# Decode attention of a hybrid decoder step: value products of two groups placed between the two halves of every second scoring

## The chip, the cores and the metric

One core of one Trainium2 chip runs the whole kernel. The metric is device time in microseconds (us); a profiled execution also has a span, from its first to its last instruction. All inputs and outputs are fp32.

## The reference, cut to what matters

The kernel computes one step of a one-layer decoder for a prompt of 1024 tokens and for 8 sample sequences of 8 new tokens each. The change touches only the latent attention of the samples. Each sequence reads 32 cache pages of 128 tokens (latent width 256, rotary width 32) through a page table, and its queries are 8 heads x 8 tokens = 64 rows:

```
def one_seq(args):
    pt, ql, qr, cn, kn = args
    ckv = concatenate([cache_ckv[layer, pt].reshape(4096, 256), cn])
    kr  = concatenate([cache_kr[layer, pt].reshape(4096, 32), kn])
    scores = (einsum("bqhc,btc->bhqt", ql, ckv) + einsum("bqhr,btr->bhqt", qr, kr)) * MLA_SCALE
    p = softmax(where(mask, scores, NEG_INF))
    return einsum("bhqt,btc->bqhc", p, ckv)
```

## The kernel before, in words

`decode_attention` (L1433) runs on all engines between the prompt's cross-attention and the samples' cross-attention (`cross_decode`). It takes the 256 pages of the 8 sequences as 64 **groups** of 4 pages, 8 groups (G) to a sequence, numbered n = 0 to 63. PE's program, L1585 to L1616, is written out by hand as 16 **steps** of 4 groups each (S = 4), n = 0, 4, ..., 60. A step scores groups n to n+3, and works off the values of the four groups from p = n - 8 on, that is of the sequence before. Two steps make a sequence: the steps with n a multiple of 8 (p % G == 0), below called **first steps**, and the others, below called **second steps**, which are the ones that the change rewrites.

The parts of PE's program:

- `scores(n, part)` (L1523): for each of 8 slices of the latent (d, 32 wide) 8 matmuls on 32x64 tiles of the array (L1535), so 64 for a half (4 slices) and 128 in all; then 16 matmuls for the rotary part (L1543), and in a second step also 4 + 2 recorded ones for the new tokens (L1549, L1550). They all add up in PSUM banks 0 to 3, and the last one raises `scored`. The first half waits for the transposed queries (`q_in`), for the scores of the step before to be out of PSUM (`s_done`) and for the turned keys (`keys_done`), L1528 to L1530.
- `turn_probs(p)` (L1553): 4 transposes (L1559) of the probabilities of groups p and p+1. It waits for their exponentials (`exped`) and for its PSUM bank (5 or 6, `pt_done`).
- `values(n)` (L1563): 4 products in the code, 8 matmul records, on L1575 (probabilities x latents, 256 columns), which add up in bank 7 (bank 0 for the last sequence) and raise `pv_done`. `pair(p)` is two of them, so 16 records; for the first pair of a sequence 2 more on L1572.
- `turn_side(j)` (L1505): the transposes of the new tokens' probabilities (L1510) and of the output of the sequence before (L1519); it waits for the first exponential of the sequence.

The order in a first step is: half of the scoring, `turn_side`, `turn_probs(p)`, the other half, `turn_probs(p + 2)`, `pair(p)`, `turn_probs(p + 4)`, `pair(p + 2)`. In a second step: all of the scoring, `turn_probs(p + 2)`, `pair(p)`, `pair(p + 2)`. In steps 0 and 4 there are no values yet. After step 60 PE goes on with `turn_side(7)` and the values of the last sequence (L1600 on).

Around it:

- DVE: `keep_scores` (L1694) takes the four groups out of PSUM (L1704) once `scored` is up, and after a second step takes the row maximum (L1712 to L1727), which raises `maxed`; `keys` (L1680) turns the latents of later groups (L1032, L1041) as their pages land.
- ACT: `exps` (L1642, instructions L1649) makes the exponentials in place after `maxed`; `probs` (L1634, L1639) copies turned probabilities out of PSUM; `finish` (L1652, L1655) takes a sequence's output out once all its values are done (`pv_done`), ahead of the exponentials of the next sequence in ACT's queue.
- POOL (L1803): after the scoring of step n it gathers the pages of groups n+8 to n+11, one indirect DMA of 512 KB each (`gather_pages`, L1057), and then two groups' rotary keys (`gather_rotary`, L1076). The first gather waits for `scored` of step n; each page gather also waits for `pv_done` of the group whose slot it overwrites (19 slots).
- SP (L1480): the other rotary keys, the queries of the sequence after next, and at the end the first loads of the stages behind, after `scored` or `pv_done`.

Of the kernel before, what the change touches and what calls it, by code (L numbers as in the profile page):

```python
# [990 lines left out]
G = NPAGES // 4  # L991
# [31 lines left out]
def key_slot(n):  # L1023

    return (n + S) % (2 * S)
# [407 lines left out]
def decode_attention(nc, ps, a, k, at, e, late, clear_old):  # L1433
# [3 lines left out]
    NB = KVL // 32  # L1437
# [16 lines left out]
    def probs_at(p):  # L1454

        return 5 + p // 2 % 2, pt[:, p // 2 % 2]
# [7 lines left out]
    with ExitStack() as c:  # L1464
# [39 lines left out]
        def _(pe):  # L1504
            def turn_side(j):  # L1505

                if j:
                    pe.wait_ge(side_kept, j)
                pe.wait_ge(exped, j * (G + 1) + 1)
                last = pe.transpose(ps[0:NS, SIDE, 0:R], sn[:, j % 2, :], k["ident"][0:R, 0:R])  # L1510
                if 0 < j < DECB - 1:
                    last = turn_out(j - 1)
                last.then_inc(side_turned, 1)
# [9 lines left out]
            def scores(n, part):  # L1523
                b, new = n // G, n % G == G - S
                x = key_slot(n)
                cols = lambda i, f: ps[f * R:(f + 1) * R, i, 0:S * 64].rearrange("p (x w a) -> p x a w", x=S, a=2)
                if 0 in part:
                    pe.wait_ge(q_in[b % 2], 64 * (b // 2 + 1))  # L1528
                    pe.wait_ge(s_done, item(b, n % G))
                    pe.wait_ge(keys_done, n // 2 + 2)  # L1530
                for d in part:
                    for f in range(2):
                        for i in range(4):
                            rows = slice(32 * i, 32 * (i + 1))
                            pe.matmul(cols(i, f), q_rows[rows, b % 2, d, :],  # L1535
                                             kT[rows, x:x + S, 2 * f:2 * f + 2, d, :], start=(d == 0), stop=False,
                                             tile_position=(32 * i, f * R))
                if NB - 1 not in part:
                    return
                for f in range(2):  # L1540
                    for i in range(4):
                        rows = slice(32 * i, 32 * (i + 1))
                        last = pe.matmul(cols(i, f), qrope[rows, b, :], rT[rows, x:x + S, 2 * f:2 * f + 2, :],  # L1543
                                         start=False, stop=not (new and i == 0 and f == 0),
                                         tile_position=(32 * i, f * R))
                if new:
                    o = ps[0:R, 0, S * 64:S * 64 + NS]
                    for t in range(CT):
                        pe.matmul(o, qlat[:, t, b, :], k["cnT"][:, t, :], start=False, stop=False)  # L1549
                    last = pe.matmul(o, qrope[0:ROPE, b, :], k["krT"][:, :], start=False, stop=True)  # L1550
                last.then_inc(scored, 1)

            def turn_probs(p):  # L1553

                pe.wait_ge(exped, p // G * (G + 1) + 3 + p % G)
                if p >= 4:
                    pe.wait_ge(pt_done, p // 2 - 1)
                for w in range(4):
                    last = pe.transpose(ps[:, probs_at(p)[0], w * P:(w + 1) * P], sc[:, (p + w // 2) % NSC, w % 2:HK:2],  # L1559
                                        k["ident"][:, :])  # L1560
                last.then_inc(p_turned, 1)

            def values(n):  # L1563
                b, g = n // G, n % G
                pe.wait_ge(pt_done, n // 2 + 1)
                to, held = acc(b), probs_at(n - n % 2)[1]
                if g == 0:
                    pe.wait_ge(side_kept, b + 1)
                    if 0 < b < DECB - 1:

                        pe.wait_ge(o_normed, b)
                    pe.matmul(ps[0:R, to, 0:KVL], ptn[:, b % 2, :], k["cn"][:, :], start=True, stop=False)  # L1572
                for f in range(2):
                    for e in range(2):
                        last = pe.matmul(ps[e * R:(e + 1) * R, to, 0:KVL], held[:, n % 2, f, e * R:(e + 1) * R],  # L1575
                                         raw_c[:, n % NAT, 2 * e + f, :], start=(g == 0 and f == 0 and e == 1),
                                         stop=(g == G - 1 and f == 1))
                last.then_inc(pv_done, 1)

            def pair(p):  # L1580
                values(p)
                values(p + 1)

            pe.wait_ge(cleared, 1)
            for n in range(0, NG, S):  # L1585
                p = n - LAG
                if p >= 0 and p % G == 0:
                    scores(n, range(NB // 2))
                    turn_side(p // G)
                    turn_probs(p)  # L1590
                    scores(n, range(NB // 2, NB))
                else:
                    scores(n, range(NB))
                if p >= 0:
                    turn_probs(p + 2)
                    pair(p)
                    if p % G == 0:
                        turn_probs(p + 4)
                    pair(p + 2)
            turn_side(DECB - 1)  # L1600
            turn_probs(NG - G)
            for p in range(NG - G, NG, 2):
# [1353 lines left out]
```

## Time and profile before

| | us |
|---|---|
| three runs | 1451.31, 1457.43, 1449.00 (median 1451.31) |
| the profiled execution: its own time | 1452.62 |
| the profiled execution: span | 1450.7 |
| PE busy in the span | 1392.7 (96%), mean granted clock 0.977 |
| DVE, ACT, POOL busy | 836.3, 516.0, 245.2 |
| decode_attention in the span, by PE's first and last rows | 429.5 to 665 |

The rows below are of the profiled execution, in microseconds from the span's start. A timeline row merges neighbouring instructions of one line and form: start, length to the last end, engine, line, operation, out<-in, count. Where work follows without a gap, the cost of a row is the start of the next row less its own start, since matmuls are pipelined and their ends overlap what follows.

### The profile page before, as it was taken

Reading aid. Unit: us, or ns where it says so; the run is one execution under the profiler, and the core shown is the slowest. Engines: PE = TensorE matmul, PEld = TensorE weight load, DVE = VectorE, ACT = ScalarE, POOL = GpSimd, SP = SyncE. Lnnn points to the kernel's source line nnn. Section 1 sums busy time; section 2 is a strip of 40 time slices with the busy share of each in tenths; the row PEclk is TensorE's granted clock in tenths of the full one; section 3 lists DMA queues with packets and bytes.
Section 4 is the critical chain, followed back from the end, with each engine's and each line's share of the span. In section 5 each row is a group of like instructions: output and inputs, shape, how many; then the busy total and the mean of one; then the engine's idle time right before and its main releaser. Section 6 shows DMA issues by size and latency. Waiting matters only on the chain.

```text
span 1450.7 us, 28032 instructions
## 1 busy us (share of the span) xinstructions
PE 1392.7 (96%) x11192; PEld 1218.5 (84%) x11192; DVE 836.3 (58%) x1615; ACT 516.0 (36%) x1102; POOL 245.2 (17%) x193
## 2 busy tenths in 40 slices
PE   7999999999988899898999999999999999999997
PEld 7998977777646555565999999999999999999885
DVE  3385356776676445555575676664444445567745
ACT  4321456665351222234424333443333343113100
POOL 3110037764642433410100000000000000000000
PEclk9999999999999888999899999999999999999999
DMA  6652020001372545649313113133333327452722
GB/s 235 194 158 93 1 88 1 1 1 55 130 243 65 180 147 171 214 164 380 106 44 90 45 45 89 45 90 95 106 101 115 96 93 271 167 196 72 263 87 73
DMA packets 108437, 174.37 MB, mean 120 GB/s; under 512 B 14002, under 2 KB 77298, under 8 KB 107028
## 3 DMA queue, kind: packets, MB, share of 16 engines
q1 hardware_dynamic: 98068, 136.92, 28.7%
q0 software_dynamic: 10240, 35.66, 7.2%
q8 instruction: 89, 1.46, 0.4%
q14 instruction: 40, 0.33, 0.1%
HBM read 138.49 MB, written 34.06 MB: 119 GB/s over the span
## 4 chain that ended last, share of the span: by engine, by line
PE 52%; DVE 0%; issue 0%; ACT 0%; DVEq 0%
PE ps L2462 35%; PE ps L2493 10%; PE ps L2527 6%; PE ps L2513 0%; DVE p_h L2835 0%; DVE p_h L2838 0%; DVE p_stats L2822 0%; DVE p_h L2818 0%; PE ps L2503 0%; DVE p_mv L2829 0%; ACT p_rt L2610 0%; DVE p_rs L2833 0%; DVE p_stats L2827 0%; DVE p_stats L2826 0%; DVE p_ve L2831 0%
## 5 line engine op out<-in xcount | busy, mean ns | idle before, releaser
L2462 PE MATMUL ps<-p_x,p_w 128*128 128x272 f32 x4032 | 508.7, 289 | 1.0 <-PEq L1993 0.7
L2462 PEld LDWEIGHTS ps<-p_x,p_w 128*128 128x128 f32 x4032 | 508.4, 189 | 1.5 <-issue 1.5
L2493 PE MATMUL ps<-p_uh,p_w 128*128 128x352 f32 (+1 forms) x576 | 141.9, 327 | 0.0
L987 POOL TENSOR_SCALAR p_pr<-p_pr,p_rec 128x896 f32<-128x896 f32 (+3 forms) x64 | 109.8, 1725 | 141.6 <-DVE p_rec L951 141.4
L2712 DVE TENSOR_TENSOR p_w<-p_sum,p_w 128x512 fp32r<-128x512 f32 x94 | 65.0, 691 | 119.2 <-ACT p_w L1920 119.0
L1535 PE MATMUL ps<-p_kT,p_q_rows 32*64 32x256 f32 x2048 | 104.9, 452 | 23.0 <-issue 18.7
L1535 PEld LDWEIGHTS ps<-p_kT,p_q_rows 32*64 32x64 f32 x2048 | 63.4, 157 | 60.7 <-issue 54.2
L1920 ACT ACTIVATE p_w<-p_wr 128x512 fp32r<-128x512 f32 x96 | 60.1, 626 | 131.4 <-PE ps L2493 76.0
L2493 PEld LDWEIGHTS ps<-p_uh,p_w 128*128 128x128 f32 x576 | 101.8, 188 | 0.0
L1032 DVE STREAM_TRANSPOSE p_kT<-p_rawc 128x1024 f32<-128x1024 f32 x64 | 77.7, 1232 | 38.1 <-DMA p_rawc<-cache_ckv,p_rows 37.3
L2493 PE MATMUL ps<-p_ul,p_w 128*128 128x352 f32 (+1 forms) x288 | 94.4, 328 | 0.0
L2712 DVE TENSOR_TENSOR p_w<-p_wr,p_w 128x512 fp32r<-128x512 f32 x95 | 65.6, 690 | 38.5 <-ACT p_w L1920 38.0
L1057 POOL DMA_INDIRECT p_rawc<-cache_ckv,p_rows x64 | 65.3, 1020 | 126.8 <-PE ps L1543 45.1
L1920 ACT ACTIVATE p_w<-p_sum 128x512 fp32r<-128x512 f32 x96 | 59.8, 623 | 18.5 <-PE ps L2462 11.9
L945 DVE TENSOR_REDUCE p_nmax<-ps 128x1 f32<-128x896 f32 (+3 forms) x64 | 48.1, 752 | 25.9 <-PE ps L833 24.7
L1704 DVE CUSTOM_DVE_ANT_0 p_sc<-ps,p_zero 128x256 f32<-128x256 f32 x64 | 23.3, 421 | 66.0 <-PE ps L1543 52.4
L1575 PE MATMUL ps<-p_rawc,p_pt 128*64 128x256 f32 x512 | 60.5, 384 | 0.0
L2493 PEld LDWEIGHTS ps<-p_ul,p_w 128*128 128x128 f32 x288 | 54.1, 188 | 0.0
L1639 ACT ACTIVATE p_pt<-ps 128x512 f32<-128x512 f32 x28 | 16.7, 597 | 99.3 <-PE ps L1559 99.3
L1575 PEld LDWEIGHTS ps<-p_rawc,p_pt 128*64 128x64 f32 x512 | 34.6, 137 | 20.0 <-issue 3.1
L899 ACT ACTIVATE p_pr<-ps,p_nmax 128x896 f32<-128x896 f32 (+3 forms) x64 | 47.4, 740 | 5.5 <-DVE p_nmax L945 4.7
L2546 ACT ACTIVATE p_slots<-p_slots 128x544 f32<-128x544 f32 x36 | 23.8, 661 | 70.5 <-PE ps L2462 70.5
(338 smaller groups left out, 2483.3 us busy)
## 6 DMA issues: line engine op xcount, KB each, us to landing
p_wr<-w_in SPq DMA_DIRECT2D x48, 512.0 KB, 3.6
g_kept<-p_slots SPq DMA_DIRECT2D x48, 272.0 KB, 2.5
p_ring<-g_kept SPq DMA_DIRECT2D x16, 544.0 KB, 4.3
p_x<-x_kept SPq DMA_DIRECT2D x6, 1088.0 KB, 7.5
t_kept<-p_t_raw SPq DMA_DIRECT2D x16, 272.0 KB, 2.4
p_x<-t_kept SPq DMA_DIRECT2D x4, 1088.0 KB, 8.5
p_gy<-g_kept SPq DMA_DIRECT2D x8, 544.0 KB, 5.5
p_xs<-x_prompt SPq DMA_DIRECT2D x8, 512.0 KB, 4.2
```

What stands on the lines that cost most here:

```text
L899: nc.scalar.activation(pr[:, n % PR, 0:w], src[:, 0:w], ACT.Exp, bias=nmax[:, n % PR:n % PR + 1], accum_out=tot[:, n % PR:n % PR + 1]).the ...
L945: dve.tensor_reduce(nmax[:, n % PR:n % PR + 1], src[:, 0:w], AX, ALU.max, negate=True).then_inc(maxed, 1)
L987: nc.gpsimd.tensor_scalar(pr[:, n % PR, 0:w], pr[:, n % PR, 0:w], rec[:, n % PR:n % PR + 1], None, ALU.mult).then_inc(normed, 1)
L1032: return dve.transpose(e["kT"][:, key_slot(n)].rearrange("p a d w -> p (a d w)"), e["raw_c"][:, s].rearrange("p a c -> p (a c)"))
L1057: nc.gpsimd.indirect_dma_start(e["raw_c"][:, n % NAT, :, :].rearrange("p a c -> p (a c)"), None, rows_in, bass.IndirectOffsetOnAxis(e["row ...
L1535: pe.matmul(cols(i, f), q_rows[rows, b % 2, d, :], kT[rows, x:x + S, 2 * f:2 * f + 2, d, :], start=(d == 0), stop=False, tile_position=(32 ...
L1575: last = pe.matmul(ps[e * R:(e + 1) * R, to, 0:KVL], held[:, n % 2, f, e * R:(e + 1) * R], raw_c[:, n % NAT, 2 * e + f, :], start=(g == 0 ...
L1920: nc.scalar.activation(e["w"][:, q % NW, 0], w_source(e, q), ACT.Copy).then_inc(e["w_hi"], 1)
L2462: last = pe.matmul(ps[:, lo + z, 0:PW], w[:, q % NW, part, t, :], v[:, t, z * PW:(z + 1) * PW], start=(i in STARTS and t == 0 and n == 0), ...
L2493: last = pe.matmul(ps[:, BANK_OF[g % 8], 0:tn], w[:, q % NW, part, t, :], v[:, t0:t0 + tn], start=(t == 0 and z == 0), stop=(t == KH - 1 a ...
L2527: last = pe.matmul(ps[0:r, 2 * (i % 2) + half, :], v, o[t][:, half * BANK:(half + 1) * BANK], start=(t == 0 and q == 0), stop=(t == KT - 1 ...
L2712: dve.tensor_tensor(w[:, q % NW, 1], w_source(e, q), f32(w[:, q % NW, 0]), ALU.subtract).then_inc(w_lo, 1)
```

## The change

In second steps (p >= 0 and p % G == 4) the scoring is cut into its two halves, and `turn_probs(p + 2)` and `pair(p)` stand between them; `pair(p + 2)` stays behind. Nothing else moves: first steps, steps 0 and 4, and all other engines' programs are as before. No instruction is added or taken away.

```diff
@@ -1589,14 +1589,18 @@
                     turn_side(p // G)
                     turn_probs(p)
                     scores(n, range(NB // 2, NB))
+                    turn_probs(p + 2)
+                    pair(p)
+                    turn_probs(p + 4)
+                    pair(p + 2)
+                elif p >= 0:
+                    scores(n, range(NB // 2))
+                    turn_probs(p + 2)
+                    pair(p)
+                    scores(n, range(NB // 2, NB))
+                    pair(p + 2)
                 else:
                     scores(n, range(NB))
-                if p >= 0:
-                    turn_probs(p + 2)
-                    pair(p)
-                    if p % G == 0:
-                        turn_probs(p + 4)
-                    pair(p + 2)
             turn_side(DECB - 1)
             turn_probs(NG - G)
             for p in range(NG - G, NG, 2):
```

## Rows read from the trace of the kernel before

**Rows 1.** The page: granted clock of PE in 40 slices of 36.3 us, in tenths.
```profile
PEclk9999999999999888999899999999999999999999
```

**Rows 2.** Timeline of PE, steps 56 and 60: a stretch with few gathers, then none.
```profile
632.81 1.98 PE L1535 MATMUL ps<-p_kT,p_q_rows 32*64 32x256 f32 x64
634.58 0.64 PE L1543 MATMUL ps<-p_rT,p_qrope 32*64 32x256 f32 x16
...
638.95 1.95 PE L1575 MATMUL ps<-p_rawc,p_pt 128*64 128x256 f32 x16
640.83 3.71 PE L1535 MATMUL ps<-p_kT,p_q_rows 32*64 32x256 f32 x128
644.33 0.64 PE L1543 MATMUL ps<-p_rT,p_qrope 32*64 32x256 f32 x16
```

**Rows 3.** Timeline of all engines behind the scoring of step 60.
```profile
645.53 0.74 PE L1559 MATMUL ps<-ident,p_sc 128*128 128x128 f32 x4
...
646.21 3.67 PE L1575 MATMUL ps<-p_rawc,p_pt 128*64 128x256 f32 x32
...
648.98 0.49 ACT L1649 ACTIVATE p_sc<-p_sc,p_nmax 128x256 f32<-128x256 f32 x1
...
649.81 0.24 PE L1510 MATMUL ps<-ident,p_sn 64*64 64x64 f32 x1
...
649.98 1.36 PE L1559 MATMUL ps<-ident,p_sc 128*128 128x128 f32 x8
```

**Rows 4.** Timeline of PE, second step 28, from the transposes behind step 24's scoring on.
```profile
515.45 0.75 PE L1559 MATMUL ps<-ident,p_sc 128*128 128x128 f32 x4
...
521.14 1.52 PE L1535 MATMUL ps<-p_kT,p_q_rows 32*64 32x256 f32 x29
522.97 0.37 PE L1535 MATMUL ps<-p_kT,p_q_rows 32*64 32x256 f32 x1 [0.31 <-issue]
...
525.12 4.16 PE L1535 MATMUL ps<-p_kT,p_q_rows 32*64 32x256 f32 x96 [0.15 <-issue]
529.05 0.66 PE L1543 MATMUL ps<-p_rT,p_qrope 32*64 32x256 f32 x16
...
530.27 0.75 PE L1559 MATMUL ps<-ident,p_sc 128*128 128x128 f32 x4
```

**Rows 5.** Timeline of PE, and one row of ACT, from step 20's scoring to step 24's first half.
```profile
499.17 3.67 PE L1575 MATMUL ps<-p_rawc,p_pt 128*64 128x256 f32 x32
502.78 2.10 PE L1535 MATMUL ps<-p_kT,p_q_rows 32*64 32x256 f32 x30
505.18 0.68 PE L1535 MATMUL ps<-p_kT,p_q_rows 32*64 32x256 f32 x4 [0.30 <-issue]
506.61 0.59 PE L1535 MATMUL ps<-p_kT,p_q_rows 32*64 32x256 f32 x2 [0.75 <-issue]
508.04 2.08 PE L1535 MATMUL ps<-p_kT,p_q_rows 32*64 32x256 f32 x28 [0.84 <-issue]
510.05 0.31 PE L1510 MATMUL ps<-ident,p_sn 64*64 64x64 f32 x1
...
505.20 0.47 ACT L1655 ACTIVATE p_on<-ps,p_rec 128x256 f32<-128x256 f32 x1 [5.32 <-remote]
```

**Rows 6.** Timeline of POOL: last of one series of six gathers, first and last of the next.
```profile
506.08 1.03 POOL L1076 DMA_INDIRECT p_rawr<-cache_kr,p_rows  x1 [0.30 <-issue]
516.52 1.03 POOL L1057 DMA_INDIRECT p_rawc<-cache_ckv,p_rows  x1 [9.42 <-PE ps L1543]
...
523.14 1.03 POOL L1076 DMA_INDIRECT p_rawr<-cache_kr,p_rows  x1 [0.30 <-issue]
```

**Rows 7.** Timeline of all engines, step 0: scoring beside four rotary gathers, no values.
```profile
429.45 5.14 PE L1535 MATMUL ps<-p_kT,p_q_rows 32*64 32x256 f32 x59 [1.28 <-DVE p_tots L1771]
...
434.87 3.49 PE L1535 MATMUL ps<-p_kT,p_q_rows 32*64 32x256 f32 x67 [0.28 <-issue]
```

**Rows 8.** Windows of step 24: us, busy (x) of PE, PEld, DVE, ACT, POOL, clock, DMA share, GB/s.
```profile
508.00:512.00 4.00, 3.96 (x37) 2.93 (x36) 0.03 (x1) 0.43 (x3) 0.00 (x0) 0.50 0.18 57
```

## The prediction

> **What bounds the kernel now.** I read the page first: PE is busy 96% of the span, and its clock dips only where decode_attention stands [rows 1]. So PE's program sets the end, and the question is how fast PE gets through the 16 steps. The timeline of PE where no gather runs gives clean prices. 128 scoring matmuls take 640.83 to 644.33, 3.50 us; a half of 64 takes 632.81 to 634.58, 1.77; a pair of groups' values takes 638.95 to 640.83, 1.88 [rows 2]. The 4 transposes take 645.53 to 646.21, 0.68, and two pairs of values in a row 646.21 to 649.81, 3.60 [rows 3].
>
> The same timeline in the middle is slower. In second step 28 the 128 scoring matmuls take 521.14 to 529.05, 7.91 us: 29 start at once, four come one by one some 0.7 us apart, and at 525.12 the other 96 run [rows 4]. In first step 24 the half takes 502.78 to 510.05, 7.27 us [rows 5]. No other engine is named as what ended these gaps, only "issue". POOL's rows beside them show where they come from: a series of six gathers ends at 507.11 (506.08 + 1.03), the next runs from 516.52 to 524.17 [rows 6], and PE is free 0.93 and 0.95 us after the last one ends (508.04, 525.12). I looked at eleven such steps; the gap closes 0.8 to 1.0 us behind POOL's last gather in each.
>
> The starts in those rows run ahead of the work. The last values before step 24's scoring end by 502.84 (499.17 + 3.67), yet ACT's L1655, which waits for them, starts at 505.20 [rows 5], when PE's record has 30 scoring matmuls started. So about 32 matmuls stand between the recorded start and completion when PE is held. The Trainium skill (TensorE: Matmul & The Clock Gate, the table of the array) gives a queue of 64 instructions, which would be 32 loads and 32 matmuls; the row agrees.
>
> With that I count what PE completes from the end of one scoring until it is free. Behind a first step: 515.45 to 525.12, 9.67 us; started 4 + 2 + 16 + 4 + 16 + 32 (29 + 3 single), so completed about 42. Behind a second step: from 0.68 before 499.17 to 508.04, about 9.6 us; started 4 + 32 + 36, completed about 40 [rows 5]. In clean time the first lot is worth 5.7 us and the second 4.4, but the counts agree: **while POOL issues gathers, PE is limited in matmuls, not in their length**, to 4 or 5 per us. Step 0 says the same without values and with hardly any page traffic: 59 scoring matmuls started, so about 27 completed, from 429.45 to 434.87, in 5.4 us, 5 per us [rows 7]. Under a gather a scoring matmul (0.027 us clean) costs 0.2 us; a value matmul (0.11 us) nearly the same.
>
> **The change, part by part.** It moves one `turn_probs` and one `pair` of each second step from behind `scored` to before it, in 7 steps (12, 20, ..., 60). No DMA is moved and no queue passed on SP or POOL; POOL's series starts on `scored`, so it now starts later.
>
> 1. Ahead of `scored`. Up to the first scoring matmuls of a second step nothing changes: the series behind the first step stands over the same 42 matmuls, and the held stretch ends where it did, with matmul 0 or 1 of the scoring. The moved work comes after, where nothing hides it: 0.68 + 1.88, and 0.04 for cutting the scoring (2 x 1.77 less 3.50) [rows 2, 3]: **+2.60 us** a step.
> 2. Behind `scored`. Before, 4 + 32 matmuls and the first 5 or so of the next half stood under the series. Now 16 values do, and then scoring matmuls. PE is free no earlier, since the series has the same six gathers. In the 1.07 us before POOL starts (515.45 to 516.52) [rows 4, 6] PE does some 9 values, then 8.5 us at 4 to 5 per us: 43 to 51 completed, so 27 to 35 scoring matmuls instead of 4 or 5. That is 23 to 30 fewer afterwards, at 0.027 each clean, or 0.033 as in step 24 (508.04 to 510.05 for the last 60, part of it at half clock) [rows 5]: 0.6 to 1.0, **-0.8 us**. 20 hidden values and transposes are traded for scoring matmuls that would have been short anyway.
> 3. Net +1.8 us a sequence, in the 6 second steps (12 to 52) with a series behind them (of five gathers behind step 52): **+10.8 us**.
> 4. Step 60 has no gathers. Its own sum is 2.60 less the 2.40 that leave (4.28 less 1.88): +0.2. But behind it `turn_probs(56)` needs the second group's exponential, whose instruction (648.98 + 0.49) and its accumulator read end 4.0 us after the scoring's end at 645.53. PE now comes there 4.45 us after it (649.98) and waits for nothing [rows 3]. With only 1.88 us of values and 0.17 of L1510 between, it comes at 2.05 and waits 2.0, and the transposes after it wait for later exponentials 0.5 us apart, another 0.2. **+2.2 us**, so +2.4 with its own sum.
>
> Waits that tighten elsewhere: the next first step's `s_done` wait has only 1.88 us of values in front of it, and `turn_side` the exponentials' 4.0 us; both fall under the series, where PE is held anyway, and become real only if the hold goes. `turn_probs(p + 2)` comes 1.7 us or more earlier but its exponentials are made before the scoring starts, so nothing. DVE keeps its order; its keys land with the gathers, ahead of use.
>
> Sum: +13.2 us on the profiled execution's 1452.6, 1465.8. The median of the runs shown is 1.3 lower, so **1464.5 us**. The bounds of part 2: at worst nothing is got back (2.60 a sequence, +18 in all, 1469); at best everything that left counts (0.2 a sequence, +3.6 in all, 1455). I take the count, because step 0 and both kinds of step agree on it.
>
> A page speaks against the change in its own way. The values and the scoring use other tilings of the array, and the change adds two switches a step. In the rows, cutting a run of values in two costs 0.16 us (2 x 1.88 less 3.60), cutting the scoring 0.04 [rows 2, 3]; that is inside my prices. The Trainium skill (TensorEngine Tiling, Key Properties) says that changing the mode drains TensorE. If each drain showed in full, as 0.37 us, the length of one scoring record [rows 4], 14 of them would add 5 us: 1469.
>
> **The rivals.**
> - *PE is slowed in proportion, not in number.* Then what leaves the series' stretch is made up by what enters it: +0.2 a sequence and the 2.4 at the end, 1454. For it: the stretch behind a first step got through 5.7 us of clean work, so what is long is not always held long. Against it: step 0. 0.25.
> - *Only the value matmuls are slowed,* because they read the tiles into which the pages land. Then fewer of them under the series is a gain: the next `scored` could come with POOL's last gather, 8.7 us (515.45 to 524.17) behind the scoring, where it takes 17.0 now (498.49 to 515.45) [rows 4 to 6]; less 2.6 that is 5.7 us a sequence, 34 less in all, 2.4 more at the end: 1420. For it: in step 28 the matmuls that hold on are the last values. Against it: step 0 has no values and is held, and in step 24 four or five scoring matmuls are held too. It decides if step 24's half ends within 4 us of its start. The Trainium skill (SBUF — State Buffer, Who interferes with whom) says that DMA never contends with a compute engine; by that rule this rival, and any gain, falls. 0.12.
> - *The clock.* PE runs at 0.50 of the clock, 1.2 GHz of 2.4, from 508 to 512, just behind the held stretch, in which few matmuls ran [rows 5, 8]. With scoring matmuls instead of values under the series it is idler for longer. If each sequence has another such 4 us, that is 2 us x 6 on top: 1476. 0.08.
> - *Drains as above,* 1469. 0.05.
>
> **How the numbers follow.** The forecast has 0.50. Half a per cent is 7.3 us, about what a measurement of this kernel can tell from no change. By that the forecast, the clock and the drains are slower, but for the forecast's low side of 0.03: 0.60. The proportional case and most of that low side are within: 0.27. Values only, and a little from waits that I don't see, is faster: 0.13. The range goes from 1450, a little under the proportional case, to 1473, the worst of part 2 with a few us of clock or drains; the gain and the far end of the clock case stay out.
>
> **What would show it.** In the changed profile: (1) in second steps the scoring's first 29 or so matmuls, then the one-by-one starts, end as before, and L1559 and L1575 (16) follow them, clean; scored to scored over a second step grows from 14.8 (515.45 to 530.27) to about 17.4 [rows 4]. (2) In first steps the half starts 1.9 us behind the scoring's end, is held until 0.9 us behind POOL's last gather, with 60 or more started instead of 36. (3) Behind step 60, L1510 or the L1559 after it stands idle 1 to 2 us, ended by ACT L1649. I am wrong if scored to scored over a first step shrinks by 2.4 us or more (proportional), or by far more (values only).

## The result, and the profile after

The changed kernel takes 1477.3 us (median of 4 runs, 1473.07 to 1478.14) beside 1451.23 for the kernel before: ratio 1.0173, 95% interval 1.0143 to 1.0203, so 26 us slower. The forecast was 13 us slower, 1464.5, with a range to 1473: the sign was right, the size half of what it is. The profiled execution of the changed kernel has a span of 1475.0 us (before 1450.7) and a mean granted clock of 0.971 (before 0.977).

The timeline of PE in the changed kernel, second step 28, is to be read beside [rows 4], then the first half of first step 24 beside [rows 5]:

```profile
518.31 0.74 PE L1559 MATMUL ps<-ident,p_sc 128*128 128x128 f32 x4
...
523.99 1.71 PE L1535 MATMUL ps<-p_kT,p_q_rows 32*64 32x256 f32 x30
526.46 1.10 PE L1535 MATMUL ps<-p_kT,p_q_rows 32*64 32x256 f32 x4 [0.76 <-issue]
527.92 2.07 PE L1535 MATMUL ps<-p_kT,p_q_rows 32*64 32x256 f32 x30 [0.36 <-issue]
529.92 1.13 PE L1559 MATMUL ps<-ident,p_sc 128*128 128x128 f32 x4
530.98 2.08 PE L1575 MATMUL ps<-p_rawc,p_pt 128*64 128x256 f32 x16
532.99 1.98 PE L1535 MATMUL ps<-p_kT,p_q_rows 32*64 32x256 f32 x64
```

The held stretch stands where it stood: 30 scoring matmuls start, then four more, and at 527.92, 9.61 us behind the scoring before, PE is free (9.67 before). What the change moved, the L1559 and L1575 at 529.92 and 530.98, comes after it and is paid in full.

```profile
503.83 3.76 PE L1535 MATMUL ps<-p_kT,p_q_rows 32*64 32x256 f32 x50 [0.18 <-issue]
508.36 0.66 PE L1535 MATMUL ps<-p_kT,p_q_rows 32*64 32x256 f32 x5 [0.76 <-issue]
509.78 1.09 PE L1535 MATMUL ps<-p_kT,p_q_rows 32*64 32x256 f32 x5 [0.77 <-issue]
511.22 1.13 PE L1535 MATMUL ps<-p_kT,p_q_rows 32*64 32x256 f32 x4 [0.34 <-issue]
512.27 0.31 PE L1510 MATMUL ps<-ident,p_sn 64*64 64x64 f32 x1
...
514.41 3.54 PE L1535 MATMUL ps<-p_kT,p_q_rows 32*64 32x256 f32 x64
517.77 0.61 PE L1543 MATMUL ps<-p_rT,p_qrope 32*64 32x256 f32 x16
```

In this first step, whose series follows the scoring's end at 501.71, 60 scoring matmuls have started by 510.9 instead of 36, as forecast, and L1510 stands 10.56 us behind the scoring, where it stood 11.55 behind (498.50 to 510.05): 1.0 us was gained. But the second half now takes 514.41 to 517.77, 3.36 us. Before, in the same step, it took 2.72:

```profile
512.19 2.90 PE L1535 MATMUL ps<-p_kT,p_q_rows 32*64 32x256 f32 x64
514.91 0.61 PE L1543 MATMUL ps<-p_rT,p_qrope 32*64 32x256 f32 x16
```

Clean it takes 1.77, so both kernels lose time here, and the changed one more: its granted clock from 512 to 516 is 0.50, where before it is 0.50 from 508 to 512 [rows 8] and 0.73 from 512 to 516. Of the 1.0 us only 0.35 is left at `scored` (16.60 us from the scoring before, instead of 16.95). The windows from one `scored` to the next show how it came out in every step. They run from step 12's `scored` to step 60's, first steps and second steps in turn; columns: us, busy (x) of PE, clock, DMA share, GB/s. Before, the first pair and the last:

```profile
466.10:483.26 17.16, 15.28 (x191) 0.81 0.46 154
483.26:498.50 15.24, 13.58 (x200) 0.88 0.50 160
...
622.35:635.15 12.80, 11.70 (x191) 1.00 0.54 171
635.15:645.53 10.38, 10.38 (x200) 1.00 0.59 218
```

After (the three left out are like those above them: 16.55 at 0.79, 17.63 at 0.90, 16.56 at 0.79):

```profile
467.05:483.85 16.80, 14.79 (x172) 0.80 0.48 154
483.85:501.71 17.86, 16.37 (x221) 0.90 0.41 139
501.71:518.31 16.60, 14.25 (x171) 0.79 0.48 155
518.31:535.97 17.66, 16.40 (x221) 0.90 0.44 139
...
586.71:606.36 19.65, 17.68 (x221) 0.83 0.42 136
606.36:623.57 17.21, 15.54 (x171) 0.70 0.57 211
623.57:641.32 17.75, 16.01 (x220) 0.90 0.40 131
641.32:655.17 13.85, 12.48 (x172) 0.88 0.50 158
655.17:668.29 13.12, 13.12 (x221) 1.00 0.47 172
```

The six windows of second steps grow from 83.82 us in all to 103.67, +19.85; the six of first steps from 95.61 to 97.57, +1.96. A window's length times (1 - clock) is what half clock takes from it at most (half of the time spent at 0.50): 13.6 us in the six first-step windows of before and 20.6 after, 6.9 and 10.4 in the second steps (the windows of before that are left out have 16.95 us at 0.80, 14.82 at 0.88, 15.81 at 0.89, 15.00 at 0.89, 15.78 at 0.89, 13.52 at 1.00, 17.11 at 0.80 and 14.86 at 0.89). That is 10.5 us more, and the forecast had none of it.

The end, behind step 60's scoring, beside [rows 3]:

```profile
668.29 1.95 PE L1575 MATMUL ps<-p_rawc,p_pt 128*64 128x256 f32 x16
671.48 0.21 PE L1510 MATMUL ps<-ident,p_sn 64*64 64x64 f32 x1 [1.25 <-ACT p_sn L1653]
672.37 0.74 PE L1559 MATMUL ps<-ident,p_sc 128*128 128x128 f32 x4 [0.68 <-ACT p_sc L1653]
673.35 0.74 PE L1559 MATMUL ps<-ident,p_sc 128*128 128x128 f32 x4 [0.24 <-ACT p_sc L1653]
674.03 0.64 PE L1572 MATMUL ps<-cn,p_ptn 64*64 64x256 f32 x2
674.60 3.63 PE L1575 MATMUL ps<-p_rawc,p_pt 128*64 128x256 f32 x16
678.16 0.66 PE L1519 MATMUL ps<-p_pair_id,p_on 128*128 128x64 f32 x4
```

PE waits 1.25 + 0.68 + 0.24 = 2.2 us for ACT's exponentials (L1653 is the L1649 of before; the change shifts lines behind it by 4), which is the forecast's wait to the tenth. The pair at 674.60 then takes 3.56 us, 1.7 more than clean, at half clock again.

### The profile page after: what moved, and what is told of

It is laid out like the page before. It is cut to its first block, busy times and chain, and to the rows that moved or that the text cites. A ratio compares the mean times of both kernels' runs of the same rounds, so it can differ in the third digit from the quotient of the medians.

```text
span 1475.0 us, 28032 instructions
## 1 busy us (share of the span) xinstructions
PE 1411.7 (96%) x11192; PEld 1218.6 (83%) x11192; DVE 836.3 (57%) x1615; ACT 516.1 (35%) x1102; POOL 244.7 (17%) x193
## 4 chain that ended last, share of the span: by engine, by line
PE 51%; DVE 0%; issue 0%; ACT 0%; DVEq 0%
PE ps L2466 34%; PE ps L2497 10%; PE ps L2531 6%; PE ps L2517 0%; DVE p_h L2839 0%; DVE p_h L2842 0%; DVE p_stats L2826 0%; DVE p_h L2822 0%; PE ps L2507 0%; DVE p_mv L2833 0%; ACT p_rt L2614 0%; DVE p_stats L2831 0%; DVE p_rs L2837 0%; DVE p_ve L2835 0%; DVE p_stats L2830 0%
## 5 line engine op out<-in xcount | busy, mean ns | idle before, releaser
L1535 PE MATMUL ps<-p_kT,p_q_rows 32*64 32x256 f32 x2048 | 118.4, 461 | 26.1 <-issue 21.9
L1535 PEld LDWEIGHTS ps<-p_kT,p_q_rows 32*64 32x64 f32 x2048 | 62.9, 158 | 74.7 <-issue 69.0
L1575 PE MATMUL ps<-p_rawc,p_pt 128*64 128x256 f32 x512 | 66.2, 404 | 0.0
L1575 PEld LDWEIGHTS ps<-p_rawc,p_pt 128*64 128x64 f32 x512 | 35.9, 145 | 22.4 <-issue 7.5
```

The source lines that it names most:

```text
L1535: pe.matmul(cols(i, f), q_rows[rows, b % 2, d, :], kT[rows, x:x + S, 2 * f:2 * f + 2, d, :], start=(d == 0), stop=False, tile_position=(32 ...
```

## The experiments

Six batches ran, each on another chip, with the kernel before beside it. They came upon **two kinds of chip**: on three of them the kernel before takes 1450.8 to 1457.1 us, as in the trace shown, and on three 1390.4 to 1392.4. Each chip was met in one batch only, so no run tells whether the kind belongs to the chip itself or to its state at that time. Each result below stands beside the before of its own batch.

**Batch 1: POOL's gathers taken away, parts of the change alone.** In the two "sp" kernels SP loads the samples' pages and rotary keys by plain DMAs of the same size from fixed pages (the page table is left out), and POOL issues nothing in decode. `sp_before` has PE's order of before, `sp_after` that of the changed kernel:

```diff
-                        pool.wait_ge(scored, n // S + 1)
-                        pool.wait_ge(pv_done, x - NAT + 1)
-                        gather_pages(nc, a, e, x)
+                        sp.wait_ge(scored, m // S + 1)
+                        sp.wait_ge(pv_done, x - NAT + 1)
+                        load_pages(sp, a, e, x)
```

> The order of before, with all page and rotary loads of the decode stage issued by SP as plain DMAs of the same sizes, and none by POOL. It reads fixed pages instead of those of the page table, which is left out; the traffic is the same. Theory 1 (POOL's issuing of gathers holds PE): no more single starts some 0.7 us apart in L1535, a half scoring takes 1.8 to 2.0 us and a whole one 3.5 to 4 everywhere, the clock stays at 1.00, and a sequence takes 20 to 24 us instead of 31: 1390 to 1415 us in all. Theory 2 (the traffic itself holds PE): the single starts stay where DMA share is over 0.8, and the time is 1440 to 1460.

> The changed order with the same loads by SP as e1_sp_before (the page table left out in the same way). Theory 1: without a hold the moved values cost only the cuts (0.2 us a second step, 7 steps) and the wait for the exponentials, which now shows in every first step (up to 1 us) and behind step 60 (2.2 us): 3 to 10 us more than e1_sp_before. Theory 2: still 20 to 28 us more than e1_sp_before, as the change cost with gathers by POOL.

`ahead` puts in second steps the same transposes and the same pair as the change ahead of the whole scoring (the order within a second step, beside before):

```diff
+                    turn_probs(p + 2)
+                    pair(p)
                     scores(n, range(NB))
-                    turn_probs(p + 2)
-                    pair(p)
                     pair(p + 2)
```

> Second steps do the transposes and the first pair of values ahead of the whole scoring, which is not cut. Theory 1 (what counts is that 20 long matmuls leave the stretch behind the second scoring, where PE was held anyway): as slow as the changed kernel, 1470 to 1480, with scored to scored over a second step 2.5 to 3 us longer than before. Rival (the cut of the scoring is what costs, each half being held or drained by itself): within 5 us of before, 1448 to 1456.

`side_first` has in first steps `turn_side` and `turn_probs(p)` ahead of an uncut scoring, second steps as before:

```diff
-                    scores(n, range(NB // 2))
                     turn_side(p // G)
                     turn_probs(p)
-                    scores(n, range(NB // 2, NB))
+                    scores(n, range(NB))
```

> The order of before in second steps; in first steps the side transposes and turn_probs(p) come ahead of the whole scoring instead of between its halves, so that the stretch in which POOL holds PE covers 9 more long matmuls and fewer short ones. Theory 1: 1 to 2 us less a first step with gathers (the 9 are worth 1.3 us clean and 2.1 at half clock), 1440 to 1448. Rival (the wait for the exponentials, about 4 us behind the scoring, becomes the bound): 1452 to 1460, with idle time ahead of L1510 ended by ACT.

Measured, beside 1392.35 (13 runs): sp_before 1407.7, sp_after 1417.62, ahead 1396.83 (ratio 1.0032, 1.0013 to 1.0051), side_first 1411.5 (1.0143, 1.0109 to 1.0176). The before of this batch was the surprise, 59 us under the one shown, and so none of these runs could tell what the hold costs. A trace of the kernel before on such a chip (e7_before_again below) shows the same instructions with no hold. Timeline of PE, then POOL, second step of before without the hold:

```profile
495.99 3.71 PE L1535 MATMUL ps<-p_kT,p_q_rows 32*64 32x256 f32 x128
499.49 0.64 PE L1543 MATMUL ps<-p_rT,p_qrope 32*64 32x256 f32 x16
```

```profile
490.88 1.02 POOL L1057 DMA_INDIRECT p_rawc<-cache_ckv,p_rows  x1 [2.69 <-PE ps L1543]
...
497.49 1.02 POOL L1076 DMA_INDIRECT p_rawr<-cache_kr,p_rows  x1 [0.30 <-issue]
```

POOL's six gathers take as long as with the hold, 7.63 us (490.88 to 498.51; 7.65 in [rows 6]), and lie across the scoring, which takes its clean 3.50. The batch also says what the waits are worth without the hold: side_first, with PE idle 0.99 us for the exponentials and 2.35 us at the next transposes, loses 19 us.

**Batch 2: before and after once more.**

> The kernel before, once more, for its trace. It measured 1451 us at first and 1392 us beside the runs of the call before this one, on another chip. Theory 1 (the hold of PE under POOL's gathers comes and goes with the chip, not with the kernel): where it takes 1390 to 1396 us its trace has no single starts in L1535 and a whole scoring takes 3.5 us; where it takes 1449 to 1457 it has them, 3 to 5 us a step. Rival (the 59 us lie elsewhere, in the stages before or behind): the single starts are there at 1392 too.

> The changed kernel, once more, on the same chip as e4_before_again. Theory 1: where that has no hold, the change costs only the cut of the scoring and of the values (0.2 us a second step), short waits, and 1 to 3 us behind step 60: 2 to 8 us more, 1394 to 1400 beside 1392. Where it has the hold, 23 to 29 us more. Rival (the change costs the same 26 us with and without a hold): 1415 to 1420 beside 1392.

Measured on a chip with the hold: before 1451.83 beside 1452.74, the changed kernel 1477.54, ratio 1.0158 (1.012 to 1.0197). The result stands in a second measurement on such a chip, and the kernel file is not what differs between the two kinds.

The two traces of this batch are of one chip, and their windows from `scored` to `scored` can be set side by side. The six second-step windows grow from 82.70 to 102.18 us, +19.48; six times the forecast's 2.60 is 15.6, and half clock takes at most 3.7 more than before. The six first-step windows shrink from 98.72 to 96.79, -1.93, where the forecast had -4.8; half clock takes at most 3.6 more there.

**Batch 3: the parts again, and the transposes alone.** `turn_only` leaves both pairs behind the scoring and puts only the four transposes between its halves (beside the changed kernel):

```diff
                     scores(n, range(NB // 2))
                     turn_probs(p + 2)
-                    pair(p)
                     scores(n, range(NB // 2, NB))
+                    pair(p)
                     pair(p + 2)
```

> The same kernel as e1_sp_before (order of before, all loads of the decode stage by SP, fixed pages instead of the page table's), in case this call falls on a chip with the hold (kernel before at 1449 to 1457). Theory 1 (what holds PE there is POOL's issuing of gathers): 1400 to 1415, no single starts in L1535. Theory 2 (the traffic itself, on such a chip): 1440 to 1460 with single starts. On a chip without the hold: 1405 to 1412 as before, and nothing is told apart.

> The same kernel as e1_sp_after (changed order, all loads by SP, fixed pages). With the hold on this chip, theory 1: 5 to 15 us more than e5_sp_before, as the 10 us without the hold. Theory 2: 20 to 30 us more.

> The same kernel as e2_ahead (transposes and first pair of values ahead of the whole scoring in second steps). With the hold on this chip, theory 1: 1470 to 1480, as the changed kernel, because the same 20 long matmuls leave the held stretch behind the second scoring. Rival (the cut of the scoring is what costs): 1450 to 1458.

> Half the change: in second steps only turn_probs(p + 2) stands between the halves of the scoring, both pairs of values stay behind it. With the hold on this chip, theory 1: only 4 matmuls leave the held stretch, 0.7 us a step, so 3 to 8 us more than before, 1455 to 1460. Rival (the cut of the scoring is what costs): 1468 to 1478. Without the hold: within 3 us of before.

This was a chip without the hold again, before 1390.36: sp_before 1404.05, sp_after 1414.63, ahead 1393.42 (ratio 1.0033, 1.001 to 1.0055), turn_only 1391.92 (1.0007, 0.9987 to 1.0027). Where PE is not held, cutting the scoring in two and switching to transposes and back costs nothing that can be told, and the pair of values ahead of `scored` some 3 to 4.5 us. The two sp kernels differ by 10 us in batches 1 and 3. Their loads are one long queue on SP, which starts on `scored`; that a later `scored` makes the pages late is my reading, not tried by itself. How much of it the kernel with gathers would have is open.

**Batch 4: the same parts on a chip with the hold.** This is the batch that decides.

> The changed kernel as it is. Two theories. (A) What the change costs is made by the hold: on a chip whose kernel before takes about 1452 us the scoring under POOL's gathers is held and the change costs 26 us; on a chip whose kernel before takes about 1391 us there is no hold, and there the change costs only what it makes late behind step 60 and at the exponentials, 2 to 6 us (ahead, which moves still more, cost 3 to 4.5 us there). (B) The order itself costs it (switches between the scoring and the values, later gathers): then it costs 20 us or more on either kind of chip. Beside 1391: A 1393 to 1397, B 1411 or more. Beside 1452: both 1478.

> In second steps the transposes and both pairs of values stand ahead of the whole scoring. On a chip with the hold (before about 1452): by the count of matmuls it puts 4.3 us ahead of scored and gets 1.1 back behind it, 6 times, and 2 to 6 us behind step 60: 1473 to 1478 without another half-clock stretch. If the half-clock stretches behind the hold grow as they did in the changed kernel (another 2 us a sequence), 1485 to 1490. If it were the cutting of the scoring in two that costs, it would be under the changed kernel, 1460 or less. On a chip without the hold: 1394 to 1397 as before, by either.

> In second steps only the four transposes stand between the two halves of the scoring; both pairs of values stay behind. On a chip with the hold (before about 1452): 0.7 us ahead of scored for 4 hidden matmuls, so 1455 to 1457 by the count of matmuls; if the switch between the halves were the cost, most of the 26 us, 1470 or more. On a chip without the hold: 1391 to 1393.

> The kernel before with the pages of the samples loaded by SP, by plain DMAs from fixed places of the cache (the page table is left out), so POOL issues nothing in decode; the bytes are the same. On a chip with the hold (before about 1452): if POOL's indirect issuing makes the hold, the scorings take 3.50 us and the time is 1400 to 1415 as on the other chips, where SP's late loads set it; if the traffic into the tiles that PE reads makes it, the scorings are held here too and the time is 1450 or more. On a chip without the hold it takes about 1405 and tells nothing new.

| beside before 1457.1 (21 runs) | us | ratio, 95% |
|---|---|---|
| e6_after_again | 1486.64 | 1.0204 (1.0176 to 1.0232) |
| e6_ahead | 1453.36 | 0.9984 (0.9967 to 1.0001) |
| e6_turn_only | 1469.62 | 1.0084 (1.0061 to 1.0108) |
| e6_sp_before | 1405.6 | 0.9662 (0.9632 to 0.9692) |

*What holds PE.* sp_before takes 1405.6 here, 1407.7 and 1404.05 on the other kind of chip: with POOL silent the two kinds are alike. It is not the traffic either. The window 500 to 570 of sp_before on this chip (columns: PE, PEld, DVE, ACT, POOL, clock, DMA share, GB/s):

```profile
500.00:570.00 70.00, 66.39 (x1235) 45.37 (x1216) 49.37 (x129) 23.99 (x84) 0.00 (x0) 1.00 0.74 248
```

```profile
507.88 3.71 PE L1558 MATMUL ps<-p_kT,p_q_rows 32*64 32x256 f32 x128
511.38 0.64 PE L1566 MATMUL ps<-p_rT,p_qrope 32*64 32x256 f32 x16
```

The DMA engines move 248 GB/s into the same tiles, more than the 154 to 230 of before's windows up to step 60, and the scoring (L1558 and L1566 here are L1535 and L1543 of before) takes 3.50 us at full clock. So what holds PE on some chips comes with POOL's gathers and not with the amount of traffic. The sp kernels change more than the engine that issues: the kind of DMA, its queue, and the page table. Which of these matters is open, and so is whether PE, while held, cannot run what it has or does not get its instructions: the profile has only "issue" for the gaps.

*Where the moved work must stand.* ahead moves the same instructions as the change and costs nothing where the change costs 29 us. My expectation for it was worked out wrongly: I put the moved 2.56 us on the path, though by the count they go under the hold (it also speaks of both pairs; one pair is moved, as in the change). Its timeline of PE, second step 28:

```profile
514.69 0.75 PE L1559 MATMUL ps<-ident,p_sc 128*128 128x128 f32 x4
...
518.50 1.95 PE L1575 MATMUL ps<-p_rawc,p_pt 128*64 128x256 f32 x16
520.37 0.74 PE L1559 MATMUL ps<-ident,p_sc 128*128 128x128 f32 x4
521.05 1.95 PE L1575 MATMUL ps<-p_rawc,p_pt 128*64 128x256 f32 x16
522.93 0.66 PE L1535 MATMUL ps<-p_kT,p_q_rows 32*64 32x256 f32 x9
524.48 3.54 PE L1535 MATMUL ps<-p_kT,p_q_rows 32*64 32x256 f32 x116 [0.89 <-issue]
```

62 transposes and value products start at their clean spacing (514.69 to 522.93), 9 scoring matmuls start, and at 524.48 PE is free, 9.79 us behind the scoring. Started by then: 62 + 9 = 71. (3 of the 128 records are missing, so it may be 74.) In before it was 42 + 32 = 74 [rows 4], in the changed kernel 42 + 34 = 76, in turn_only 42 + 29 = 71. These 9 with their gap take 1.55 us, where 32 took 3.98 in before. The number that starts under a series of gathers is nearly fixed, and their length is free: 20 long ones more under it instead of 20 or so short ones cost nothing, and the same 20 behind it cost 2.6 us. Over the twelve windows from step 12's `scored` to step 60's, ahead takes 182.0 us, before 179.4 and the changed kernel 201.2.

Recorded starts are no measure of what is done, though. ACT copies the result of the transposes at 520.37 only at 524.60, where the same copy elsewhere starts 0.8 us behind the transposes:

```profile
518.60 0.60 ACT L1642 ACTIVATE p_pt<-ps 128x512 f32<-128x512 f32 x1 [2.53 <-PE ps L1559]
...
524.60 0.60 ACT L1642 ACTIVATE p_pt<-ps 128x512 f32<-128x512 f32 x1 [4.42 <-DMA p_wr<-w_in]
```

So under the gathers completion lags the starts by up to 3.4 us. When PE is free the lag is gone: from 524.48 to the rotary matmuls' clean place at 528.03 are 3.55 us at clock 1.00, and the 119 scoring matmuls that were left are worth 3.25, so not much more than the 9 just started was still open. The kernel before shows it without a rest in batch 2, where the clock is 1.00 throughout second step 28: 74 are started when PE is free at 525.55, and the 96 left take 2.64 us, which is their clean price.

*The clock.* The windows of ahead, first and second steps in turn (columns as above):

```profile
498.45:514.69 16.24, 14.13 (x171) 0.79 0.49 162
514.69:529.23 14.54, 13.65 (x220) 1.00 0.50 166
529.23:545.44 16.21, 14.01 (x171) 0.79 0.48 162
545.44:559.87 14.43, 13.97 (x220) 1.00 0.51 166
```

The first steps have the order of the changed kernel and its clock, 0.79. In the second steps, behind a hold that lay over 62 long matmuls, the clock is 1.00 in all five windows with gathers; in the changed kernel, 42 long ones, it is 0.90 or less in all five, as in batch 6's trace; in those of batches 2 and 4 one of the five is at 1.00 and the others are at 0.83 to 0.91. At 17.7 us a window that is 1.8 us a sequence, a third of the 29. In all, length times (1 - clock) comes to 20.4 us in ahead, as much as in before (20.4), but all of it in first steps; the four traces of the changed kernel have 29.3 to 34.0 and the two of before on such chips 20.4 and 22.0. turn_only was expected 3 to 5 us over before and takes 12.5 more. Two of its windows:

```profile
500.33:518.37 18.04, 15.94 (x188) 0.72 0.43 145
518.37:534.68 16.31, 14.54 (x204) 0.90 0.48 151
```

Over its twelve windows length times (1 - clock) comes to 27.0 us, beside 20.4 in before and 31.0 in the changed kernel: about half of the 12.5 us can be half clock. But there is no simple order in it: in first steps, turn_only with 32 long matmuls under the hold has windows of 0.72 to 0.89, the changed kernel with 16 has 0.70 to 0.88, before with 36 has 0.80 to 1.00. Only the second steps of ahead are free of it throughout.

**Batch 5: what of POOL's work holds PE, and still more ahead.** `pool_plain` replaces POOL's indirect gathers by plain DMAs that POOL issues at the same places from fixed pages (the page table is left out); `both_ahead` also puts the second pair ahead of the scoring.

```diff
-    nc.gpsimd.indirect_dma_start(e["raw_c"][:, n % NAT, :, :].rearrange("p a c -> p (a c)"), None, rows_in,
...
+    nc.gpsimd.dma_start(e["raw_c"][:, n % NAT, :, :].rearrange("p a c -> p (a c)"),
+                        a["cache_ckv"][0, 4 * n:4 * n + 4].rearrange("n (p a) c -> (n p) (a c)", a=4)
```

```diff
                     turn_probs(p + 2)
                     pair(p)
+                    pair(p + 2)
                     scores(n, range(NB))
-                    pair(p + 2)
```

> The kernel before once more, for a trace of this chip. 1450 to 1460 with the scorings under POOL's gathers at 7 to 8 us (a hold), or 1388 to 1396 with scorings of 3.50 us (none). Nothing else is expected by any theory.

> The kernel before with POOL's indirect gathers of pages and rotary keys replaced by plain DMAs of the same size, issued by POOL at the same places, from fixed pages (the page table is left out). On a chip with the hold (before about 1455): if it is the indirect descriptors, whose making occupies POOL about 1 us each, that hold PE, the scorings take 3.50 us and the time is 1385 to 1410; if anything that POOL issues holds PE, the scorings are held as now, 1440 or more. On a chip without the hold (before about 1391): 1385 to 1405, and it tells nothing.

> In second steps the transposes and both pairs of values stand ahead of the whole scoring. By the count of matmuls (about 71 starts under a series of gathers, whatever their length) 78 long ones stand ahead of the second step's scoring, so it runs unheld in 3.5 to 4.2 us, and only scoring matmuls are held behind it: 6 long ones more lie outside the held stretches than before, +0.5 us a sequence, and +2 to 6 behind step 60: on a chip with the hold +3 to +9 beside before, if the stretches at half clock stay as long as they are. If PE were slowed in proportion to the length of its work, the second step's scoring would still be held 3 us or more and the time would be 20 or more above before. If half clock comes from held scoring matmuls, the stretches stand only behind second steps' scorings and are longer there. On a chip without the hold (before about 1391): 1397 to 1403, since the exponentials are waited for in both kinds of step.

A chip without the hold: before_again 1392.04 (one run), pool_plain 1391.55 (1.001, 0.999 to 1.003), both_ahead 1408.84 (1.0123, 1.0103 to 1.0142). So whether plain DMAs from POOL would hold PE stays open, and what both_ahead does under the hold as well. both_ahead shows another price, 17 us over before instead of the 6 to 12 expected. With no values behind `scored`, the next half waits until DVE has taken the scores out of PSUM; in before the same 2.05 us stand ahead of step 8's scoring, which has no values ahead of it either, and there the profile names DVE (448.23, `[2.05 <-DVE p_gmax L1715]`). The timeline of PE in both_ahead:

```profile
530.95 0.32 PE L1550 MATMUL ps<-krT,p_qrope 32*64 32x64 f32 x2
533.33 1.16 PE L1535 MATMUL ps<-p_kT,p_q_rows 32*64 32x256 f32 x16 [2.05 <-issue]
```

2.05 us idle a sequence, where the changed kernel and ahead have 0.18, as one pair's 1.88 us just covers it.

**Batch 6: the changed kernel, for a chip without the hold.**

> The changed kernel once more, for a chip without the hold (before about 1391). By the theory that its 26 to 29 us come from the hold (long matmuls taken out of the held stretches, and the half clock that follows), it costs there about what the same work ahead of the scoring cost, 3 to 5 us: 1394 to 1398. By the theory that the order itself costs it, 20 us or more: 1411 or more. On a chip with the hold (before 1450 to 1460) both give +26 to +30 again.

The chip had the hold: 1477.57 beside 1450.77, ratio 1.0174 (1.0141 to 1.0207). The third chip of that kind gives the result again; what the changed kernel costs where PE is not held was not obtained. ahead, 3 to 4.5 us there, is the nearest.

## Why the prediction was right in its steps and wrong in its sum

- **Step 1, +2.60 us ahead of `scored`: right.** The seven second steps grow by 2.76 (step 12), 2.62, 2.84, 2.63, 6.13, 2.89 and 2.74 us. Step 44 has the 3.3 more at half clock (0.83 in its window, where before had 1.00).
- **Step 2, -0.8 us a sequence behind `scored`: the step that failed.** The difference in the count was right: 60 matmuls are started instead of 36, and L1510 comes 1.0 us earlier in step 24. But hardly any of it reached `scored`: steps 16 and 24 are 0.36 and 0.35 us shorter, the four later ones longer, and the six windows are 1.96 us longer in all instead of 4.8 shorter. The saving was priced with the clock of before, and the half clock grew, in the first steps' windows by 7.0 us of lost time at most, which is about the gap between -4.8 and +1.96 (6.8). ahead, whose first steps have the same order, has the same: 0.79 in these windows and 96.59 us instead of 95.61. In batch 2's pair on one chip the same step fails by less, -1.93 instead of -4.8.
- **Step 3, 1.8 us in each of six sequences, +10.8:** those six second and six first steps, from step 8's `scored` to step 56's, grow by 21.8 us (180.38 to 202.21).
- **Step 4, behind step 60: right.** The wait is 2.2 us. The scoring interval is longer by 2.74 us and the tail behind it by 1.44 (17.52 to 18.96 us, up to L1618, L1614 before), of which 1.7 is the pair at half clock; without that the two give 2.5, against 2.4.
- **The term that was mis-sized** is thus the clock, taken as unchanged. The half clock's share is at most 10.5 us between steps 12 and 60 and 1.7 behind, 12.2, and 12.7 were missing (decode as a whole, from step 0's first scoring matmul to L1618, grew from 233.6 to 259.5 us, by 25.9). The rival "the clock" named this and gave it 2 us a sequence and a chance of 0.08; its total of 1476 is nearest to the result. The prediction had the row for it [rows 8] and said why it should grow, but kept as a side case what its own step 2 brings about: more short matmuls under the hold leave PE emptier. ahead supports that in both kinds of step (1.00 where more long matmuls stand under the hold, 0.79 where fewer do); turn_only, with 32 long ones and up to 22.1 us lost in first steps, speaks against it, and what makes the clock fall stays open.
- **The count of what PE completes was wrong, without harm to the sum.** The prediction took 32 off the number started and had about 42 completed behind a first step, 4 to 5 per us. At the end of the hold all 74 are done (batch 2's before), in 9.62 us, which is 7.7 per us. The lag that it read from ACT's L1655 is there in the middle of the hold and not at its end. Part 2 used only the difference between two counts, which holds.
- **The rivals.** Proportional slowing (1454) falls: it wanted first steps 2.4 us shorter, they are 0.36 us shorter at best, and in ahead 62 long matmuls are through by the end of a hold of the same length. "Only the value matmuls are slowed" (1420) falls: step 24's half, which should then end within 4 us of its start, takes 8.4 (503.83 to 512.27) with 16 values under the gathers. Drains: turn_only adds the same two switches a step and costs 1.5 us (interval -1.8 to 3.8) where there is no hold, so at most 0.3 us each; no more than 3.8 of the 26 to 29 us can be theirs by that.

## What to carry to other kernels

When another engine's work limits how many instructions PE starts, and not how long they are, put the long instructions where the limit holds and the short ones behind it: the same transposes and products cost 29 us between the halves of a scoring and nothing that can be told ahead of it. Price a freed or emptied stretch of PE with the clock that will follow it, and read that from windows at both kinds of place. And look at a second chip before the mechanism of one trace is taken for the kernel's: here the stall on which the whole argument rests was worth some 60 us on three chips and absent on three others.

## What the runs showed of the hardware that was not expected

- The same kernel takes 1451 to 1457 us on three chips and 1390 to 1392 on three others. On the first kind PE is held while POOL issues indirect gathers (71 to 76 matmuls of second steps started in the 9.6 to 9.8 us), on the second a 128-matmul scoring under the same gathers takes 3.50 us. With POOL silent both give 1404 to 1408. The Trainium skill (SBUF — State Buffer, Who interferes with whom) says that PE never waits on anyone; for the tiles' traffic the runs agree (248 GB/s, no hold), but while POOL gathers, PE is held on three of the chips. Whether that is a wait at a memory port or something else no run shows, nor what makes the difference between the chips.
- The mean granted clock is under 1.00 in nine of before's eleven windows that begin with gathers and in all eleven of the changed kernel's, with stretches at 0.50 behind the hold (512 to 516). Between steps 12 and 60 that takes up to 20.4 to 22.0 us in two traces of before and 29.3 to 34.0 in four of the changed kernel. It is 1.00 in all five windows of ahead whose hold lay over 62 long matmuls.
- Completion lags PE's recorded starts by up to 3.4 us under the gathers (batch 4) and has caught up when PE is free.
